# The PV product of an encoder layer's attention with the exponentials as the stationary operand

## The reference

```
q = rope(rms(...) * g_q_head)        # (1024, 8, 96)
k = rope(rms(...) * g_k_head)        # (1024, 8, 96)
s = einsum('bqhd,bkhd->bhqk', q, k) * 96 ** -0.5
p = softmax(s, axis=-1)
att = einsum('bhqk,bkhd->bqhd', p, v)
mix = concatenate([a, att], axis=-1) @ w_out   # a: the convolution group
h = h + gm * mix
```

## Time and profile before

| | us |
|---|---|
| median of 3 runs | 2129.99 (2129.35 to 2130.52) |
| the profiled execution | 2130.77 |
| its span, first to last instruction | 2129.0 |
| TensorE busy in the span | 2025.2 |
| attention, from the first PV product to the last | about 1005 to 1299 |
| output projection (L1742) | 1300 to 1390 |

### The profile page before, as it was taken

The page is one execution under the profiler, slowest core; times in us unless marked ns, Lnnn a source line. Parts: engine busy times, 40 slices in busy tenths (PEclk is TensorE's granted clock), DMA queues, the critical chain, the costliest instruction groups (busy, mean ns, idle before and its releaser), DMA issues.

```text
span 2129.0 us, 22064 instructions
## 1 busy us (share of the span) xinstructions
PE 2025.2 (95%) x8778; PEld 1608.0 (76%) x8778; DVE 1166.4 (55%) x1433; ACT 530.8 (25%) x690; POOL 294.3 (14%) x218
## 2 busy tenths in 40 slices
PE   3999999999999999996998998999999999999998
PEld 2788788888888878984555556878888888888886
DVE  4665554445544465775889876253444334444336
ACT  3411111111111035244665542241111111111102
POOL 1000000000000000005989842000000000000001
PEclk7999999999999999997999999999999999999999
DMA  8344221122211221000000022111111101111001
GB/s 306 119 139 131 97 89 60 59 99 89 89 59 59 99 103 51 26 1 0 1 0 0 0 66 112 40 40 60 59 60 54 35 31 59 59 59 40 20 30 79
DMA packets 76600, 137.32 MB, mean 65 GB/s; under 512 B 3308, under 2 KB 56659, under 8 KB 76274
## 3 DMA queue, kind: packets, MB, share of 16 engines
q1 hardware_dynamic: 76530, 136.35, 18.4%
HBM read 127.94 MB, written 8.39 MB: 64 GB/s over the span
## 4 chain that ended last, share of the span: by engine, by line
PE 82%; DVE 8%; issue 5%; POOL 2%; ACT 2%; DMA 1%; SPq 0%; DVEq 0%; POOLq 0%; ACTq 0%
PE ps L304 46%; PE ps L350 22%; PE ps L1742 4%; PE ps L768 3%; PE ps L1653 2%; DVE cv L918 2%; DVE negmax L705 1%; PE ps L746 1%; DVE ada_acc L461 1%; DVE grow L784 1%; PE ps L719 1%; PE ps L697 1%; PE ps L414 1%; PE ps L821 1%; PE ps L491 1%
## 5 line engine op out<-in xcount | busy, mean ns | idle before, releaser
L304 PE MATMUL ps<-xh,W 128*128 128x512 f32 x3072 | 965.4, 392 | 7.1 <-DVE xl L434 5.3
L304 PEld LDWEIGHTS ps<-xh,W 128*128 128x128 f32 x3072 | 577.3, 188 | 132.2 <-issue 6.2
L304 PE MATMUL ps<-xl,W 128*128 128x512 f32 x1536 | 598.3, 390 | 0.0
L350 PE MATMUL ps<-WD,AT 128*128 128x512 f32 x1920 | 441.2, 390 | 0.0
L350 PEld LDWEIGHTS ps<-WD,AT 128*128 128x128 f32 x1920 | 360.4, 188 | 77.5 <-issue 2.9
L328 DVE TENSOR_TENSOR tmp<-ps,tmp 128x512 f32<-128x512 f32 x88 | 60.8, 691 | 554.2 <-ACT tmp L322 554.2
L304 PEld LDWEIGHTS ps<-xl,W 128*128 128x128 f32 x1536 | 288.8, 188 | 59.6 <-issue 1.7
L360 DVE TENSOR_TENSOR H<-ps,H 128x512 f32<-128x512 f32 x352 | 240.7, 689 | 152.8 <-PE ps L350 152.4
L322 ACT ACTIVATE tmp<-ps 128x512 f32<-128x512 f32 x88 | 52.6, 598 | 748.9 <-PE ps L304 746.3
L399 POOL TENSOR_SCALAR stat<-stat 128x1 f32<-128x1 f32 x32 | 8.7, 272 | 1605.1 <-ACT XS L368 826.8
L909 POOL TENSOR_TENSOR cv<-cv,prod 128x1024 f32<-128x1024 f32 x60 | 155.5, 2616 | 29.4 <-ACT prod L901 29.4
(11 more groups left out here) (191 smaller groups left out, 1694.9 us busy)
## 6 DMA issues: line engine op xcount, KB each, us to landing
ada_raw<-in_w_ada SPq DMA_DIRECT2D x56, 512.0 KB, 4.6
rawd<-in_ffn_wd SPq DMA_DIRECT2D x22, 1024.0 KB, 4.9
rawg<-in_ffn_wg SPq DMA_DIRECT2D x21, 1024.0 KB, 5.2
rawu<-in_ffn_wu SPq DMA_DIRECT2D x21, 1024.0 KB, 7.4
ada<-in_w_ada SPq DMA_DIRECT2D x8, 1024.0 KB, 14.0
H<-in_x SPq DMA_DIRECT2D x8, 512.0 KB, 6.6
h_saved_rows<-H SPq DMA_DIRECT2D x8, 512.0 KB, 3.1
wor<-in_w_out SPq DMA_DIRECT2D x8, 512.0 KB, 3.5
```

The costliest lines, as they stand in the source:

```text
L304: mm = e.matmul(ps[:, bank], W1[:, c, m, wx, kc], X[xx][:, kc, h * HALF:(h + 1) * HALF], start=(k == 0), stop=(k == 3 * KC - 1))
L350: mm = e.matmul(ps[:, 4 + k % DB], AT[:, par, c, ax, t * P:(t + 1) * P], wd[:, c, wx, h * HALF:(h + 1) * HALF], start=(n == 0), stop=(n == ...
```

## The change

PV changes its roles. For each of the four query tiles of a unit, eight products take the exponentials of 128 keys by 128 queries as the stationary operand, and V beside its 64 columns of ones, 128 keys by 128 columns, as the moving one. The result has the query on the partition; the four tiles lie side by side in PSUM bank 6. Step p now does all eight key tiles of query tile p. ScalarE's copy is gone. VectorE takes a reciprocal of 128x4 straight from PSUM and multiplies 128x4x64 straight from PSUM into `att` (`dve_pv_out`), both in step 0 of the next unit, behind that step's maximum and its remainder or tap. PV of the next unit waits for that (`pv_out`). `att` now has the query on the partition, so the output projection turns it on TensorE (`pe_turn_att`, four transposes a token tile into PSUM bank 0 or 1), and `cut_mix` reads the attention part from there; the first products of the projection are put in another order around it.

```
 def pe_pv(e, i, m, p):
     ...
-                e.wait_ge(pv_copied, i * 4 + (m - 1))
-            for kt in (2 * p, 2 * p + 1):
-                mm = e.matmul(ps[:, 6], vs[:, hp, kt], EX[(m - 1) % 2][:, kt], start=(kt == 0), stop=(kt == NT - 1))
+                e.wait_ge(pv_out, i * 4 + (m - 1))
+            for kt in range(NT):
+                mm = e.matmul(ps[:, 6, p * VA:(p + 1) * VA], EX[(m - 1) % 2][:, kt, p * P:(p + 1) * P], vs[:, hp, kt],
+                              start=(kt == 0), stop=(kt == NT - 1))
...
-        def act_pv_copy(e, i, m):
-        def dve_pv_recip(e, i, m, third):
-        def dve_pv_scale(e, i, m):
+        def dve_pv_out(e, i, m):
+            got = ps[:, 6, 0:THALF * VA].rearrange("p (t d) -> p t d", t=THALF)
+            rec = grow[:, 0:THALF].unsqueeze(2)
+            e.wait_ge(pv_mm, i * 4 + m)
+            e.reciprocal(rec, got[:, :, VH:VH + 1]).then_inc(pv_rec, 1)
+            e.wait_ge(pv_rec, i * 4 + m)
+            dst = att[:, h * THALF:(h + 1) * THALF, bass.ds(chunk * 2 + hp, 1), :].rearrange("p t a d -> p t (a d)")
+            e.tensor_tensor(dst, got[:, :, 0:VH], rec.broadcast_to([P, THALF, VH]), ALU.mult).then_inc(pv_out, 1)
...
 unit (ScalarE)
-                    if p == 0 and not (first and m < 2):
-                        act_pv_copy(e, *at(i, m - 1))
...
 unit (VectorE)
-                    if not (first and m < 2):
-                        if p < 3:
-                            dve_pv_recip(e, *at(i, m - 1), p)
-                        else:
-                            dve_pv_scale(e, *at(i, m - 1))
+                    if p == 0 and not (first and m < 2):
+                        dve_pv_out(e, *at(i, m - 1))
...
 behind the last unit (VectorE)
-            dve_pv_recip(e, TURNS, -1, 0)
-            dve_pv_recip(e, TURNS, -1, 1)
+            dve_pv_out(e, TURNS, -1)
             dve_ln_scale(e)
-            dve_pv_recip(e, TURNS, -1, 2)
-            dve_pv_scale(e, TURNS, -1)
             cut_mix(0, 0)
-            for third in range(3):
-                dve_pv_recip(e, TURNS, 0, third)
-            dve_pv_scale(e, TURNS, 0)
+            dve_pv_out(e, TURNS, 0)
+            cut_mix(1, 0)
             cut_mix(0, 1)
+            cut_mix(1, 1)
             dve_wo_lo(e, KC - 1)
...
+            def pe_turn_att(t):
+                if t < 2:
+                    e.wait_ge(pv_out, NU * TURNS)
+                    e.wait_ge(ln_dve, 2 + CC)
+                else:
+                    e.wait_ge(mix_lo, cut_place(t - 2, 1))
+                for c in range(CC):
+                    mm = e.transpose(ps[:, t % 2, c * P:(c + 1) * P],
+                                     att[:, t, 2 * c:2 * c + 2].rearrange("p a d -> p (a d)"), ident[:])
+                mm.then_inc(att_turned, 1)
...
+            for m in range(3, 2 * NT):
+                if m % 2 == 1 and m // 2 + 1 < NT:
+                    pe_turn_att(m // 2 + 1)
```

More of the change, by code:

```diff
@@ L117, in build @@
         NZ = W_IN_L // 2
+        VA = 2 * VH
         ACW = S + CONV_K + 1
@@ L128, in build @@
             [("qn", [P, NT, NHD, QK], F32), ("kn", [P, NT, NHD, NOPE], F32), ("vn", [P, NT, NHD, VH], F32),
-             ("vs", [P, 2, NT, 2 * VH], F32)],
+             ("vs", [P, 2, NT, VA], F32)],
             [("wo", [P, KC, 2, D], F32R)])
@@ L150, in build @@
             [("_g3", [P, KC, GW], F32), ("_u3", [P, KC, GW], F32), ("wkv", [P, 2, NHD * 2 * NOPE], F32R)],
[L151 removed]
+            [("slot", [P, 2, NT, QK], F32), ("qs", [P, NT, 2 * NHD], F32), ("_s2", [P, 384], F32), ("att", [P, NT, NHD, VH], F32)],
             [("wor", [P, 2, D], F32)])
@@ L237, in build @@
         s_mm, s_exp, pv_mm, pv_rec, pv_out = (sem(n) for n in ("s_mm", "s_exp", "pv_mm", "pv_rec", "pv_out"))
-        v_ok, pv_copied = sem("v_ok"), sem("pv_copied")
+        v_ok, att_turned = sem("v_ok"), sem("att_turned")
         ln_mean, ln_mm, ln_act, ln_pool, ln_dve = (sem(n) for n in ("ln_mean", "ln_mm", "ln_act", "ln_pool", "ln_dve"))
@@ L765, in pe_pv @@
                 if not (isinstance(i, int) and i == 0 and m == 1):
-                    e.wait_ge(pv_copied, i * 4 + (m - 1))
-            for kt in (2 * p, 2 * p + 1):
-                mm = e.matmul(ps[:, 6], vs[:, hp, kt], EX[(m - 1) % 2][:, kt], start=(kt == 0), stop=(kt == NT - 1))
+                    e.wait_ge(pv_out, i * 4 + (m - 1))
+            for kt in range(NT):
+                mm = e.matmul(ps[:, 6, p * VA:(p + 1) * VA], EX[(m - 1) % 2][:, kt, p * P:(p + 1) * P], vs[:, hp, kt],
+                              start=(kt == 0), stop=(kt == NT - 1))
             if p == THALF - 1:
                 mm.then_inc(pv_mm, 1)
-        def act_pv_copy(e, i, m):
[L774 to L777, removed]
-        def dve_pv_recip(e, i, m, third):
[L781 to L784, removed]
-        def dve_pv_scale(e, i, m):
+        def dve_pv_out(e, i, m):
             hp, h = (m - 1) % NU // NH, (m - 1) % NH
             chunk = i if m >= 1 else i - 1
-            e.wait_ge(pv_rec, i * 12 + 3 * m)
-            dst = att[hp * VH:(hp + 1) * VH, bass.ds(chunk, 1), h * HALF:(h + 1) * HALF].rearrange("p a q -> p (a q)")
-            e.tensor_tensor(dst, grow[0:VH, 0:HALF], grow[0:VH, HALF:D], ALU.mult).then_inc(pv_out, 1)
+            got = ps[:, 6, 0:THALF * VA].rearrange("p (t d) -> p t d", t=THALF)
[5 more added lines that the diff above has]
+            e.tensor_tensor(dst, got[:, :, 0:VH], rec.broadcast_to([P, THALF, VH]), ALU.mult).then_inc(pv_out, 1)
         def act_v(e, i, hp, first=False):
@@ L1031, in next_head, with cut_place @@
             return (i, 1) if m // NH == 0 else (i + 1, 0)
+        def cut_place(t, part):
+            return 2 * t + part + 1 if t >= 2 else 2 * part + t + 1
         def mix_src(part, t):
-            return (cv, att)[part][:, :, t * P:(t + 1) * P]
+            if part == 0:
+                return cv[:, :, t * P:(t + 1) * P]
+            return ps[:, t % 2].rearrange("p (c q) -> p c q", c=CC)
         MB = 3
@@ L1452, in _ @@
             e.wait_ge(U.mul, 8)
-            e.memset(vs[:, :, :, VH:2 * VH], 1.0).then_inc(k_ones, 1)
+            e.memset(vs[:, :, :, VH:VA], 1.0).then_inc(k_ones, 1)
             dve_tap0(e, 2, tap0)
@@ L1550, in cut_mix @@
                     e.wait_ge(s_mm, 4 * NU * TURNS)
-                if t == 0 and part == 1:
-                    e.wait_ge(pv_out, NU * TURNS)
+                if part == 1:
+                    e.wait_ge(att_turned, t + 1)
                 if t >= 2:
@@ L1556, in cut_mix @@
                 e.tensor_copy(dst, mix_src(part, t)).then_inc(mix_hi, 1)
-                e.wait_ge(mix_hi, 2 * t + part + 1)
+                e.wait_ge(mix_hi, cut_place(t, part))
                 dst = mixT[:, t % 2, LO, part * CC:(part + 1) * CC]
@@ L1734, in pe_mix @@
                     elif m == 2:
-                        e.wait_ge(pv_copied, NU * TURNS)
+                        e.wait_ge(pv_out, NU * TURNS)
                 if h == 0:
-                    e.wait_ge(mix_lo, 2 * t + 1 + part)
+                    e.wait_ge(mix_lo, cut_place(t, part))
                 for c in range(part * CC, (part + 1) * CC):
@@ L1745, in pe_mix @@
                     mm.then_inc(mix_mm, 1)
-            for m, part in ((0, 0), (1, 0), (0, 1), (1, 1)):
-                pe_mix(m, part)
-            for m in range(2, 2 * NT):
+            pe_mix(0, 0)
+            pe_mix(1, 0)
+            pe_turn_att(0)
+            pe_turn_att(1)
+            pe_mix(2, 0)
+            pe_mix(0, 1)
+            pe_mix(1, 1)
+            pe_mix(2, 1)
+            for m in range(3, 2 * NT):
+                if m % 2 == 1 and m // 2 + 1 < NT:
+                    pe_turn_att(m // 2 + 1)
                 pe_mix(m, 0)
```

4 lines of the change are left out of this document (1 added, 3 removed).

## The result

The changed kernel takes 2145.69 us in the median (four runs, 2144.55 to 2148.72), the kernel before 2130.26. The ratio is 1.0075, with a 95% interval of 1.0063 to 1.0088. The forecast was 2155.5 with a range of 2139 to 2174: slower, as said, but by 15.4 us and not by 25.

The account below looks back on a forecast made before the run. Three engines nearly in balance, with single waits deciding: 4.6 + 8.4 + 3.0 + 5.0 + 1.7 - 0.5 + 3.5 = 25.7 us on 2130.8 makes 2156.5; allowing for the median, 2155.5 was forecast, range 2139 to 2174.

Parts of the forecast that it names:

- The bound: Attention: TensorE, VectorE and GpSimdE nearly in balance, so a change's worth depends on who waits for whom at single points.
- PV itself, +4.6 at 0.112 us a pair: PV on TensorE: 64 load-and-matmul pairs cost +0.33 us a unit, counted in some 14 of 16 units.
- The rival without overlap of loads and matmuls: PV: a pair costs 0.228 us, +7.7 us in 15 units, 2267 us in all; chance 0.04.
- The new wait: Step 0: PV waits for `dve_pv_out` behind VectorE's maximum and remainder or tap; 1.4 us in even units, 3.35 in odd.
- Odd units: Five odd units with taps: the new wait eats the gain of the dropped reciprocals, 0.6 us lost each, +3.0 us.
- the same tap and remainder stand: 1131.8 + 3.30 + 0.7: End of an odd unit: tap and remainder behind the last maximum as long as before, ending at 1135.8 against 1135.15.
- the sum: All terms of the whole kernel added: 25.7 us on the profiled execution's 2130.8.
- The clock: Half clock behind the 3.35 us gaps in odd units: 1.25 us a unit in four of five, +5.0 us.
- PV at half clock hides under it: Kernel before, end of an odd unit: half-clock PV is covered by VectorE's last tap and remainder, until 1135.15.
- The last turn and the end: Last turn: later PV in (3,1) and (3,2), +1.7 us; ahead of the projection, less VectorE work, -0.5 us.
- The projection, +3.5: Output projection: eight times four transposes on TensorE at 0.11 us each, their waits met.
- The first, that the relief comes through: VectorE's relief removes the 2.81 us wait in five odd units, new waits almost unhindering; 2123.6 us; chance 0.08.

Follow-up runs that it names:

- Run 4: The changed kernel with one column of ones beside V instead of 64, so 65 moving columns instead of 128; 2250.43 us.
- Run 1: The changed kernel with `dve_pv_out` first in step 0 on VectorE, ahead of the maximum; 2115.97 us, ratio 0.9924 to the kernel before.
- run 6: The changed kernel with GpSimdE adding only 8 of 1024 columns of each convolution product, so the result is wrong; 2135.44 us.
- run 7: The changed kernel with one transpose a token tile instead of four in the output projection; 2141.01 us.
- run 2: The changed kernel with `dve_pv_out` behind the maximum but ahead of the remainder or tap; 2127.07 us, ratio 0.9984 to the kernel before.

## Why the prediction was right, and where it was off

**The bound.** Right: the engines were in balance, and single waits decided. VectorE lost work and no time was won, because the one result that TensorE waits for stood behind the tap.

**PV itself, +4.6 at 0.112 us a pair.** Right in size: the starts of its matmuls lie 0.112 us apart at the higher clock, and 16 of them show 1.95 us with latency. A later step of an even unit takes 4.08 us instead of 4.00 (from PV to PV), so 0.3 a unit. In odd units the sum counted it although, by the prediction's own working, they end with VectorE and not with TensorE. The rival without overlap of loads and matmuls fell: the 64 pairs behind the last unit take 7.31 us, where 16 of the old ones took 7.09 (timeline of the changed kernel):

```profile
1302.49 7.31 PE L770 MATMUL ps<-vs,E 128*128 128x128 f32 x64
```

With it falls, for this kernel, the sentence of the Trainium skill (TensorE: Matmul & The Clock Gate, The mechanism) that a load overlaps with matmuls in flight only when it goes to other row groups. The same section also lets a load into the background weight buffer go ahead of them, and that leaves room for what these rows show. Run 4 adds that the moving columns don't set the 0.112.

**The new wait.** Right. `dve_pv_out` was put at 0.66 us and takes 0.17 + 0.17 (the wait between) + 0.42. In the mean of the six even units PV starts 1.44 us later behind the unit's first L698 than it did before behind L697, forecast 1.4. With PV they were given 1.73 each and got 1.64. In odd units the forecast says 3.35; from the end of the first L698 to PV are 4.58 us, before 1.23, so 3.35. Run 1 takes both away and wins 29.7 us with them.

**Odd units: the mis-sized term.** With the clock and PV's share they were to cost 3.0 + 5.0 + about 1.6, and cost 2.0. The step that failed is "the same tap and remainder stand: 1131.8 + 3.30 + 0.7". The odd unit without a fall of the clock shows it (timeline, TensorE's first and VectorE's last instructions of the unit):

```profile
1161.52 0.71 PE L698 MATMUL ps<-qkT 96*128 96x512 f32 x2
...
1176.58 1.22 DVE L706 TENSOR_REDUCE negmax<-ps 128x1 f32<-128x1024 f32 x1
1177.72 2.21 DVE L911 SCALAR_TENSOR_TENSOR cv<-ac,cw,cv 128x1024 f32<-128x1024 f32 x1
1179.96 0.68 DVE L735 TENSOR_TENSOR qkT<-ps,qkT 1x512 fp32r<-1x512 f32 x1
```

The last maximum ends 15.57 us behind the first L698, which is what the forecast has (1131.8 less 1116.22). But the tap behind it took 2.21 and not 3.30, so that the remainder ends 1.2 earlier than forecast: 0.5 less than before, not 0.65 more.

Why it took 2.21 is in the traces too. GpSimdE's additions lie beside the last tap in both kernels. Before, the second of these two begins at 1131.01 and ends at 1133.35,

```profile
1127.72 5.63 POOL L909 TENSOR_TENSOR cv<-cv,prod 128x1024 f32<-128x1024 f32 x2
```

and the tap, begun at 1131.14, ends 1.09 later, at 1134.44. In the changed kernel two of them end at 1136.27 and 1139.88,

```profile
1133.89 2.38 POOL L902 TENSOR_TENSOR cv<-cv,prod 128x1024 f32<-128x1024 f32 x1 [1.76 <-ACT prod L894]
1137.50 2.38 POOL L902 TENSOR_TENSOR cv<-cv,prod 128x1024 f32<-128x1024 f32 x1 [1.24 <-ACT prod L894]
```

and the taps begun at 1135.14 and 1138.75 end 1.08 behind each. Every tap of both kernels' attention that begins beside such an addition ends 1.08 or 1.09 us behind it, and so does the one of run 6 behind L852 (1011.58, then 1012.66). What a tap takes is thus 1.08 and what is left of GpSimdE's instruction when the tap begins. Before, the addition beside the last tap had begun 0.13 us ahead of it; in the changed kernel, where the additions wait for ScalarE's products, 1.25 us ahead of it.

So the exchange of waits was a gain of 0.9 a unit (19.6 us without a fall of the clock, where three of the five before took 20.5, each with one), not a loss of 0.6. With PV's share that is 1.8 a unit and 9 us for five, most of the 12.2 by which the sum was above the 13.5 of the span; the clock, below, takes 2.2 of it back. That the forecast still came near is in part that these two errors have opposite signs.

**The clock.** Half right. It fell in four of five odd units, as said. But a fall cost 1.5 to 1.7 (21.1 to 21.3 against 19.6 us) and 2.4 where it lasted 6.8 us, 7.2 in all instead of 5.0. "PV at half clock hides under it", for the kernel before, holds but in part. PV of step 3 kept TensorE until 1135.66, half a us behind the end of the remainder at 1135.15 (timeline of the kernel before):

```profile
1135.66 0.60 PE L821 MATMUL ps<-ident,slot 128*96 128x128 f32 x4
```

Odd units before took 19.85 us without a fall, 20.5 with one of 3.4 us, and 21.9 in unit (2,3), where it lasted 6.8. Without a fall on either side an odd unit has gained 0.3 us through the change and not 0.9.

**The last turn and the end.** 1.7 - 0.5 were forecast, -0.2 came (+0.5 and -0.7). The 0.5 of unit (3,1) is as said. The 1.4 from (3,2) did not arrive: the wait is there (2.40 us in the trace), but the reciprocals that had stood between maxima and weight splitting are gone, and the wait before the row fell from 2.31 to 0.84.

**The projection, +3.5.** Right: 3.8, and run 7 gives 0.11 a transpose.

**The rivals.** The first, that the relief comes through, was the other side of the same coin: put 2123.6, it is 2116 as soon as the release stands first (run 1). Its condition, all new waits together under some 6 us, was too strict: in run 2 twelve waits of 0.9 make 10.8 and still leave a gain of 3 us. That a VectorE instruction with two operands in SBUF contends with GpSimdE, which would spare the new multiplication (the Trainium skill, GPSIMD Engine Reference, 1. Specifications), agrees with the trace: L785 took 0.42 us all sixteen times, beside an addition or not.

## What to carry to other kernels

When an engine comes to wait for another, look at what stands ahead of the release in that other's list: here 0.8 us of work, twelve times, cost 30 us because it stood behind a maximum and a remainder or a tap, though idle time lay right ahead of them. Relief of a busy engine is worth what the last wait says, and that changes with the rest: the reciprocals alone were worth 16 us, and together with the scaling between 5 and 10 beside the new wait. A gap on TensorE can cost half its length once more through the clock (1.6 us behind 3.2), if TensorE is the last engine behind it, and less if another one is (0.6 in the kernel before).

## What the hardware showed that had not been expected

Narrow matmuls behind full loads run at the same pace but hold the clock down. With 65 moving columns instead of 128 and 0.112 us a pair in both cases, the clock mostly stayed at its lower level for 21 to 38 us at a time behind gaps after which it had been low for 3.4 to 6.8, and the kernel took 105 us more. Columns of ones that nobody reads paid for themselves.

A tap of VectorE on SBUF takes 1.27 us alone. Begun during one of GpSimdE's additions it ends 1.08 us after that addition, up to 3.30 us in all, so its price depends on when it comes. A GpSimdE instruction of 128x8 (L840 in the changed kernel) left it at 1.27.
